# A two-column matmul of zeros ahead of each run of matmuls on the weights' low parts

## The chip, the cores and the metric

The kernel runs on one core of a Trainium2 chip. The metric is the device time of one execution in microseconds (us), from the first to the last instruction and a little around them; lower is better. Engines are named as in the profile: PE is TensorE's matmul side, PEld its weight loads (LDWEIGHTS), DVE is VectorE, ACT ScalarE, POOL GpSimd, SP the engine that issues most DMAs.

## The reference, cut to what matters

Two layers of a decoder trunk over 256 tokens and a model width of 2048. All products with weight matrices are in float32.

```
for l in range(DEPTH):                       # DEPTH = 2
    h = rms_norm(x, pre_mix_norm[l])
    p = h @ w_in[l]                          # 2048 x 5648: q, k, v, z, xbc, dt
    A = attention(q, k, v)                   # 8 heads x 128, causal, 256 tokens
    S = ssd_scan(silu(conv(xbc)), dt, ...)   # 16 heads x 64, state 128
    y = concat(rms_norm(A), rms_norm(S * silu(z))) @ w_out[l]     # 2048 x 2048
    x = x + rms_norm(y, post_mix_norm[l])
    h = rms_norm(x, pre_mlp_norm[l])
    h = square(relu(h @ w_up[l])) @ w_down[l]                     # 2048 x 8192, 8192 x 2048
    x = x + rms_norm(h, post_mlp_norm[l])
```

## The kernel before, in words

Every float32 value that goes through a large product is split in two parts: a high part (`w_hi`, `a_hi`, `u_hi`), rounded to TensorE's narrower float32 kind, and a low part that holds what the rounding left (`w_lo`, `a_lo`, `u_lo`). A product is then three: high weights by high activations, high weights by low activations, low weights by high activations, all added in PSUM.

The weights stream in as chunks of 128 x 1024 numbers, eight chunks to a block of 512 output columns, 47 blocks to a layer. SP loads a chunk into `raw`, ACT rounds it to `w_hi` (L549, semaphore `hi_ready`), DVE subtracts to make `w_lo` (L1288, semaphore `split_done`), PE multiplies and counts up `mm_done`, which frees the place. Four chunks are in flight (`RING`).

PE has three ways to work off a chunk:

- `token_chunk` (lines 832 to 834): activations are the stationary operand and 512 weight columns move past. High and low take turns, 128x512 each time. Blocks of v, z, w_out and w_down.
- `half_chunk` (L888, L895) for the q and k blocks and two of xbc, and `wide_chunk` (L937, L945) for the w_up blocks: the two-width blocks. The weights are stationary, 128x128 at a time, and the activations move. `a_both` holds the high and the low part of the activations side by side, so one matmul of 512 moving columns does high weights by both (L888, L937). The low weights need the high activations alone, 256 moving columns (L895, L945). A chunk has eight matmuls of each width.
- `feature_chunk`, for the first block of a layer.

In the two-width blocks an even chunk does its 8 wide matmuls first and then its 8 narrow ones; an odd chunk does narrow first and then wide. So PE alternates between 16 wide and 16 narrow matmuls. Each matmul has a weight load of its own, 128 columns. An even chunk waits for `split_done` (`take`) between its two halves.

Other work for PE (transposes, the state-space and attention products) is placed between the chunks by a table of slots; in the q, k and xbc blocks it often stands behind an even chunk, which cuts a run of 16 narrow matmuls into 8 and 8. The table and all other engines' programs are in a fixed order.

`wdt_both` is a tile of 608 columns of the narrower float32 kind: 512 hold the parts of the dt columns of w_in, and the last 96 are zeros, written once at the start by POOL.

Of the kernel before, what the change touches and what calls it, by code (L numbers as in the profile page):

```python
# [41 lines left out]
KT = D // P  # L42
# [3 lines left out]
SH, SP_, SG, SN, TAPS = 16, 64, 2, 128, 4  # L46
# [89 lines left out]
def trunk(nc, x, positions, pre_mix_norm, post_mix_norm, pre_mlp_norm, post_mlp_norm, w_in, conv_w,  # L136
          conv_b, dt_bias, a_log, d_skip, attn_out_norm, ssd_out_norm, w_out, w_up, w_down, out):
    ctx = ExitStack()
    with ctx:
        def sb(name, shape, dt=F32):  # L140
            return ctx.enter_context(nc.sbuf_tensor(name, shape, dt))
# [19 lines left out]
        wdt_both = sb("wdt_both", [P, 2 * KT * SH + P - 2 * SH], F32R)  # L161
# [30 lines left out]
        wide = [ctx.enter_context(nc.psum_tensor(f"wide{i}", [P, 4, CB], F32)) for i in range(2)]  # L192
# [82 lines left out]
        def chunk(b, c):  # L275

            return b * NC + c
# [534 lines left out]
        def _(pe):  # L812
# [9 lines left out]
            def take(b, c):  # L822

                pe.wait_ge(sem["split_done"], RING + 1 + chunk(b, c))
# [15 lines left out]
            def feature_chunk(c, par, first_ready=None, hi_ready=None, lo_ready=None):  # L840
# [32 lines left out]
                                        skip_group_check=True)  # L873
                ins.then_inc(sem["mm_done"], 1)

            def half_chunk(c, b):

                k, c4 = divmod(c, NC // 2)
                banks = acc[1 - k]

                def w(a, kk, m):
                    return a[:, c % RING, kk * SEQ + m * P:kk * SEQ + (m + 1) * P]

                def high_weights():
                    for kk in range(2 * CK):
                        kt = c4 * 2 * CK + kk
                        for m in range(2):
                            ins = pe.matmul(banks[m], w(w_hi_off, kk, m), a_both[:, kt].rearrange("p a s -> p (a s)"),  # L888
                                            start=(kt == 0), stop=(kt == KT - 1), skip_group_check=True)
                    return ins  # L890

                def low_weights():
                    for kk in range(2 * CK):
                        for m in range(2):
                            ins = pe.matmul(banks[m][:, 0:SEQ], w(w_lo_off, kk, m), a_hi[:, c4 * 2 * CK + kk],  # L895
                                            start=False, stop=False, skip_group_check=True)
                    return ins

                if c % 2 == 0:
                    pe.wait_ge(sem["hi_ready"], chunk(b, c) + 1)  # L900
                    high_weights()
                    take(b, c)
                    ins = low_weights()
                else:
                    take(b, c)
                    low_weights()
                    ins = high_weights()
                ins.then_inc(sem["mm_done"], 1)

            def wide_chunk(c, j, b, first_ready=None, hi_ready=None, lo_ready=None):  # L910


                def w(a, kk, m):
                    return a[:, c % RING, kk * CB + m * P:kk * CB + (m + 1) * P]

                if lo_ready:
                    take(b, c)
                    for kk in range(CK):
                        k = c * CK + kk
                        pe.wait_ge(*(hi_ready if kk else first_ready))  # L920
                        for m in range(CB // P):
                            pe.matmul(wide[j][:, m, 0:SEQ], w(w_hi_off, kk, m), a_hi[:, k], start=(k == 0), stop=False,
                                      skip_group_check=True)
                            pe.matmul(wide[j][:, m, 0:SEQ], w(w_lo_off, kk, m), a_hi[:, k], start=False, stop=False,
                                      skip_group_check=True)
                    pe.wait_ge(*lo_ready)
                    for kk in range(CK):
                        for m in range(CB // P):
                            ins = pe.matmul(wide[j][:, m, SEQ:2 * SEQ], w(w_hi_off, kk, m), a_lo[:, c * CK + kk],
                                            start=False, stop=False, skip_group_check=True)  # L930
                    ins.then_inc(sem["mm_done"], 1)
                    return
                def high_weights():
                    for kk in range(CK):
                        k = c * CK + kk
                        for m in range(CB // P):
                            ins = pe.matmul(wide[j][:, m], w(w_hi_off, kk, m), a_both[:, k].rearrange("p a s -> p (a s)"),  # L937
                                            start=(k == 0), stop=(k == KT - 1), skip_group_check=True)
                    return ins

                def low_weights():
                    for kk in range(CK):
                        k = c * CK + kk
                        for m in range(CB // P):
                            ins = pe.matmul(wide[j][:, m, 0:SEQ], w(w_lo_off, kk, m), a_hi[:, k], start=False, stop=False,  # L945
                                            skip_group_check=True)
                    return ins

                if c % 2 == 0:
                    pe.wait_ge(sem["hi_ready"], chunk(b, c) + 1)
                    high_weights()
                    take(b, c)
                    ins = low_weights()
                else:
                    take(b, c)
                    low_weights()
                    ins = high_weights()
                ins.then_inc(sem["mm_done"], 1)  # L960

            for l in range(DEPTH):
# [201 lines left out]
                for slot in range(MIX_SLOTS):  # L1164
# [18 lines left out]
                    if b == 0:  # L1183
                        feature_chunk(c, 0, *(() if slot else first_waits(0)))
                    elif b < B_V:
                        half_chunk(c, l * NB + b)
                    elif b < B_OUT:
                        token_chunk(c, acc[b % 2], a_hi, a_lo)
                    else:
                        last_half = slot >= MIX_SLOTS - NC // 2  # L1190
                        token_chunk(c, acc[b % 2], u_hi, u_lo, (0,) if last_half else range(TT))
                        if slot == MIX_SLOTS - 1:

                            for c in range(NC // 2, NC):
                                token_chunk(c, acc[b % 2], u_hi, u_lo, (1,))
# [31 lines left out]
                def up_pair(q, i):  # L1227
                    for j in range(2):
                        first = j == 0 and is_first(q, i)
                        if first:  # L1230
                            first_turns(1, WARM_UP, M[3])
                            pe.wait_ge(*left(l, B_OUT + 2, 2))
                            pe.wait_ge(*left(l, B_OUT + 3, 2))
                        pe.wait_ge(*up_left(l, j, q * (QB // 2) + i, 0))
                        pe.wait_ge(*down_left(l, j, q * (QB // 2), 0))
                        for c in range(NC):
                            b = l * NB + q * (2 * QB) + i * 2 + (B_MLP + j)
                            hi_first = first and c == 0
                            if not hi_first:
                                pe.wait_ge(*upto("xT_ready", l, 8 + c + 1))  # L1240
                            wide_chunk(c, j, b, *(first_waits(1) if hi_first else ()))
                            if first:
                                for jj in NORM_PE.get(c, ()):
                                    x_turn(1, jj)
# [551 lines left out]
```

## Time and profile before

| | before |
|---|---|
| median of 3 runs | 2194.89 us (2194.66 to 2195.25) |
| the profiled execution | 2195.13 us |
| its span, first to last instruction | 2193.4 us |
| PE busy | 2174.4 us (99%), 11454 matmuls |
| PEld busy | 1867.7 us (85%), 11454 loads |
| DVE busy | 1360.5 us (62%) |
| ACT busy | 1022.7 us (47%) |
| DMA engines | 404.30 MB, mean 184 GB/s |
| granted TensorE clock | 0.999 of full speed, the 2.4 GHz level |

Matmuls overlap: one of 512 columns is shown as 389 ns long, but the next starts some 227 ns after it. So the durations say little of the rate, and starts are to be compared: in the timeline a row that merges n equal instructions begins at the start of the first, and the row of what follows on the same engine begins n steps later. The profile before and after it is one execution each; its own time is compared with its own span.

### The profile page before, as it was taken

Reading aid. Unit: us, or ns where it says so; the run is one execution under the profiler, and the core shown is the slowest. Engines: PE = TensorE matmul, PEld = TensorE weight load, DVE = VectorE, ACT = ScalarE, POOL = GpSimd, SP = SyncE. Lnnn points to the kernel's source line nnn. Section 1 sums busy time; section 2 is a strip of 40 time slices with the busy share of each in tenths; the row PEclk is TensorE's granted clock in tenths of the full one; section 3 lists DMA queues with packets and bytes.
Section 4 is the critical chain, followed back from the end, with each engine's and each line's share of the span. In section 5 each row is a group of like instructions: output and inputs, shape, how many; then the busy total and the mean of one; then the engine's idle time right before and its main releaser. Section 6 shows DMA issues by size and latency. Waiting matters only on the chain.

```text
span 2193.4 us, 32256 instructions
## 1 busy us (share of the span) xinstructions
PE 2174.4 (99%) x11454; PEld 1867.7 (85%) x11454; DVE 1360.5 (62%) x1633; ACT 1022.7 (47%) x1313; POOL 112.7 (5%) x107
## 2 busy tenths in 40 slices
PE   8999999999999999999999999999999999999998
PEld 8888888888888888888898888888888888888886
DVE  6977464764555465556588875657555655554655
ACT  6544464643444344344455444546434434443443
POOL 2051000000000000000001510000000000000000
PEclk9999999999999999999999999999999999999999
DMA  6655556656665656665556555556666566656564
GB/s 211 181 153 166 159 187 197 191 177 207 184 195 195 190 180 202 191 189 190 182 157 184 152 172 149 198 182 188 205 193 192 172 209 176 204 194 192 174 206 148
DMA packets 232312, 404.30 MB, mean 184 GB/s; under 512 B 12492, under 2 KB 61924, under 8 KB 231716
## 3 DMA queue, kind: packets, MB, share of 16 engines
q1 hardware_dynamic: 230420, 396.47, 58.7%
q10 hardware_dynamic: 1264, 5.31, 0.6%
q0 software_dynamic: 544, 1.38, 0.3%
q8 instruction: 56, 0.92, 0.2%
q14 instruction: 28, 0.23, 0.0%
HBM read 401.01 MB, written 2.10 MB: 184 GB/s over the span
## 4 chain that ended last, share of the span: by engine, by line
PE 94%; DVE 3%; issue 1%; POOL 1%; ACT 1%; DMA 0%; POOLq 0%; DVEq 0%; ACTq 0%
PE wide L937 21%; PE wide L832 16%; PE wide L834 16%; PE wide L833 16%; PE wide L945 11%; PE wide L888 6%; PE wide L895 3%; DVE w_lo L1288 1%; PE wide L869 1%; PE wide L871 1%; PE wide L872 1%; PE wide L1075 1%; PE wide L976 1%; POOL u_lo L500 0%; POOL u_hi L500 0%
## 5 line engine op out<-in xcount | busy, mean ns | idle before, releaser
L1288 DVE TENSOR_TENSOR w_lo<-raw,w_hi 128x1024 fp32r<-128x1024 f32 x752 | 923.5, 1237 | 709.1 <-ACT w_hi L549 664.3
L549 ACT ACTIVATE w_hi<-raw 128x1024 fp32r<-128x1024 f32 x752 | 788.2, 1058 | 893.0 <-PE wide L834 488.0
L832 PE MATMUL wide<-w_hi,u_hi 128*128 128x512 f32 x1280 | 498.5, 389 | 0.0
L834 PE MATMUL wide<-w_hi,u_lo 128*128 128x512 f32 x1280 | 498.0, 389 | 0.0
L833 PE MATMUL wide<-w_lo,u_hi 128*128 128x512 f32 x1280 | 497.9, 389 | 0.0
L937 PE MATMUL wide<-a_both,w_hi 128*128 128x512 f32 x2032 | 486.3, 391 | 0.0
L937 PEld LDWEIGHTS wide<-a_both,w_hi 128*128 128x128 f32 x2032 | 373.2, 188 | 72.1
L834 PEld LDWEIGHTS wide<-w_hi,u_lo 128*128 128x128 f32 x1280 | 240.2, 188 | 50.0
L833 PEld LDWEIGHTS wide<-w_lo,u_hi 128*128 128x128 f32 x1280 | 240.3, 188 | 49.7
L832 PEld LDWEIGHTS wide<-w_hi,u_hi 128*128 128x128 f32 x1280 | 240.2, 188 | 49.6
L945 PEld LDWEIGHTS wide<-a_both,w_lo 128*128 128x128 f32 x2032 | 257.3, 189 | 9.6
L945 PE MATMUL wide<-a_both,w_lo 128*128 128x256 f32 x2032 | 261.1, 281 | 0.0
L888 PE MATMUL wide<-a_both,w_hi 128*128 128x512 f32 x768 | 186.4, 393 | 0.0
L888 PEld LDWEIGHTS wide<-a_both,w_hi 128*128 128x128 f32 x768 | 140.4, 188 | 27.7 <-issue 1.0
L895 PEld LDWEIGHTS wide<-a_both,w_lo 128*128 128x128 f32 x768 | 100.0, 189 | 6.1 <-issue 1.0
L895 PE MATMUL wide<-a_both,w_lo 128*128 128x256 f32 x768 | 103.5, 282 | 0.0
L832 PE MATMUL wide<-w_hi,a_both 128*128 128x512 f32 x256 | 102.6, 401 | 0.0
L834 PE MATMUL wide<-w_hi,a_both 128*128 128x512 f32 x256 | 100.0, 391 | 0.0
L833 PE MATMUL wide<-w_lo,a_both 128*128 128x512 f32 x256 | 99.8, 390 | 0.0
L480 POOL TENSOR_TENSOR st<-st,minus_half 128x1 f32<-128x1 f32 x8 | 4.4, 547 | 1539.3 <-DVE st L1368 1539.3
L768 ACT ACTIVATE u_hi<-wk 128x512 f32 (+1 forms) x64 | 39.5, 632 | 49.5 <-DVE wk L1696 49.5
L1690 DVE TENSOR_TENSOR wk<-wide,wk 128x512 f32<-128x512 f32 x64 | 41.2, 686 | 31.8 <-ACT wk L760 31.8
(248 smaller groups left out, 1367.1 us busy)
## 6 DMA issues: line engine op xcount, KB each, us to landing
raw<-in_w_up SPq DMA_DIRECT2D x256, 512.0 KB, 3.8
raw<-in_w_down SPq DMA_DIRECT2D x256, 512.0 KB, 4.5
raw<-in_w_in SPq DMA_DIRECT2D x176, 512.0 KB, 3.7
raw<-in_w_out SPq DMA_DIRECT2D x64, 512.0 KB, 4.4
zg<-in_post_mix_norm ACTq DMA_DIRECT2D x2, 1024.0 KB, 4.7
zg<-in_post_mlp_norm ACTq DMA_DIRECT2D x2, 1024.0 KB, 7.5
out<-x_sb SPq DMA_DIRECT2D x8, 256.0 KB, 2.5
x_sb<-in_x ACTq DMA_DIRECT2D x2, 512.0 KB, 8.6
```

The costliest lines, as they stand in the source:

```text
L549: act.activation(w_hi[:, c % RING], raw[:, c % RING], ACT.Copy).then_inc(sem["hi_ready"], 1)
L768: act.activation(u.rearrange("p k s -> p (k s)"), wk[:, 2 + k], ACT.Copy)\
L832: pe.matmul(o, sh, wh, start=(k == 0), stop=False)
L833: pe.matmul(o, sh, wl, start=False, stop=False)
L834: ins = pe.matmul(o, sl, wh, start=False, stop=(k == KT - 1))
L869: pe.matmul(o(m), w(w_hi, kk, m), a_hi[:, k], start=(k == 0 and m % 2 == 0), stop=False, skip_group_check=True)
L888: ins = pe.matmul(banks[m], w(w_hi_off, kk, m), a_both[:, kt].rearrange("p a s -> p (a s)"), start=(kt == 0), stop=(kt == KT - 1), skip_gr ...
L895: ins = pe.matmul(banks[m][:, 0:SEQ], w(w_lo_off, kk, m), a_hi[:, c4 * 2 * CK + kk], start=False, stop=False, skip_group_check=True)
L937: ins = pe.matmul(wide[j][:, m], w(w_hi_off, kk, m), a_both[:, k].rearrange("p a s -> p (a s)"), start=(k == 0), stop=(k == KT - 1), skip_ ...
L945: ins = pe.matmul(wide[j][:, m, 0:SEQ], w(w_lo_off, kk, m), a_hi[:, k], start=False, stop=False, skip_group_check=True)
L1288: dve.tensor_tensor(lo[:, c % RING], raw[:, c % RING], hi[:, c % RING].bitcast(F32), ALU.subtract).then_inc(sem["split_done"], 1)
L1690: dve.tensor_tensor(wk[:, k].rearrange("p (m s) -> p m s", m=2), wide[j][:, 2 * k:2 * k + 2, 0:SEQ], wk[:, k].rearrange("p (m s) -> p m s" ...
```

## The change

A helper `add_zero` issues one more matmul. Both operands are the same two columns of zeros of `wdt_both`, so the result is a 2 x 2 block of zeros, added to two rows and two columns of a PSUM bank that the running product already uses; what is computed stays the same. It is called for every even chunk of the two-width blocks, behind the 8 wide matmuls and behind the wait for `split_done`, ahead of the first narrow matmul.

```
+            def add_zero(bank):
+
+                zero = wdt_both[:, 2 * KT * SH:2 * KT * SH + 2]
+                pe.matmul(bank[0:2, 0:2], zero, zero, start=False, stop=False, skip_group_check=True)
+
             def half_chunk(c, b):
...
                     pe.wait_ge(sem["hi_ready"], chunk(b, c) + 1)
                     high_weights()
                     take(b, c)
+                    add_zero(banks[0])
                     ins = low_weights()
...
                     high_weights()
                     take(b, c)
+                    add_zero(wide[j][:, 0])
                     ins = low_weights()
```

PE's order of work in the first half block (the xbc block behind the first one) of a layer, before: L1006 and L1007 are the dt product, L888 the wide and L895 the narrow matmuls, L1014 a transpose.

```order
L1006 MATMUL wide<-a_both,wdt_both 128x256
L1007 MATMUL wide<-a_both,wdt_both 128x256
L888 MATMUL wide<-a_both,w_hi 128x512 x8
L895 MATMUL wide<-a_both,w_lo 128x256 x16
L888 MATMUL wide<-a_both,w_hi 128x512 x16
L895 MATMUL wide<-a_both,w_lo 128x256 x8
L1014 MATMUL wide<-ident,wk 128x128 x2
L895 MATMUL wide<-a_both,w_lo 128x256 x8
```

The same place now; all lines below `add_zero` have moved by 5 to 7 (L893 is the wide matmul, L900 the narrow one, L879 the new one):

```order
L1013 MATMUL wide<-a_both,wdt_both 128x256
L1014 MATMUL wide<-a_both,wdt_both 128x256
L893 MATMUL wide<-a_both,w_hi 128x512 x8
L879 MATMUL wide<-wdt_both 2x2
L900 MATMUL wide<-a_both,w_lo 128x256 x16
L893 MATMUL wide<-a_both,w_hi 128x512 x16
L879 MATMUL wide<-wdt_both 2x2
L900 MATMUL wide<-a_both,w_lo 128x256 x8
L1021 MATMUL wide<-ident,wk 128x128 x2
L900 MATMUL wide<-a_both,w_lo 128x256 x8
```

Nothing changes places; one matmul with its own weight load comes in ahead of each run, and where other work cuts a run in two, ahead of its first part alone. The same holds in the w_up blocks, here at the turn from one block to the next (PSUM tile wide0 to wide1; L943 wide, L951 narrow):

```order
L943 MATMUL wide0<-a_both,w_hi 128x512 x16
L879 MATMUL wide0<-wdt_both 2x2
L951 MATMUL wide0<-a_both,w_lo 128x256 x16
L943 MATMUL wide0<-a_both,w_hi 128x512 x8
L943 MATMUL wide1<-a_both,w_hi 128x512 x8
L879 MATMUL wide1<-wdt_both 2x2
L951 MATMUL wide1<-a_both,w_lo 128x256 x16
```

A layer has 6 half blocks with 4 even chunks each, and 16 w_up blocks with 4 each; in one of the latter, the first of the layer, the first chunk has another form without the new matmul. That makes 24 + 63 = 87 a layer and 174 in all. Followed through the program's order, 26 of the 48 in the half blocks and 2 of the 126 in the w_up blocks stand ahead of a run that other work cuts after its first 8 matmuls; the other 146 stand ahead of 16. No other engine's instructions change.

## Rows read from the trace of the kernel before

**Rows 1.** The page: busy time and instructions; then the chain's shares.
```profile
PE 2174.4 (99%) x11454; PEld 1867.7 (85%) x11454; DVE 1360.5 (62%) x1633; ACT 1022.7 (47%) x1313; POOL 112.7 (5%) x107
...
PE 94%; DVE 3%; issue 1%; POOL 1%; ACT 1%; DMA 0%; POOLq 0%; DVEq 0%; ACTq 0%
```

**Rows 2.** Waits of PE, longest first: us in total, times, longest us.
```profile
PE wide L819 <- DMA wk<-in_ssd_out_norm: 2.6, 1, 2.6
```

**Rows 3.** Groups: line, engine, operation, count | busy, mean ns | idle before.
```profile
L937 PE MATMUL wide<-a_both,w_hi 128*128 128x512 f32 x2032 | 486.3, 391 | 0.0
L945 PE MATMUL wide<-a_both,w_lo 128*128 128x256 f32 x2032 | 261.1, 281 | 0.0
```

**Rows 4.** Timeline of PE, w_up block, a wide run: start, us, engine, line, operation, count.
```profile
749.45 3.82 PE L937 MATMUL wide<-a_both,w_hi 128*128 128x512 f32 x16
753.10 2.05 PE L945 MATMUL wide<-a_both,w_lo 128*128 128x256 f32 x16
```

**Rows 5.** Timeline of both sides at one change from wide to narrow.
```profile
747.34 0.41 PEld L945 LDWEIGHTS wide<-a_both,w_lo 128*128 128x128 f32 x2
747.56 0.40 PE L945 MATMUL wide<-a_both,w_lo 128*128 128x256 f32 x2
```

**Rows 6.** Timeline of PEld, loads for matmuls of 64 moving columns.
```profile
137.19 0.97 PEld L1075 LDWEIGHTS wide<-x_tok,wk 128*128 128x128 f32 x8 [1.37 <-DVE wk L1541]
138.08 0.19 PEld L1062 LDWEIGHTS wide<-u_hi,low 128*128 128x128 f32 x1
```

**Rows 7.** Timeline of PEld, loads for matmuls of 16 moving columns and the next.
```profile
71.02 0.30 PEld L1022 LDWEIGHTS wide<-dts,tri 128*128 128x128 f32 x2
71.24 0.30 PEld L888 LDWEIGHTS wide<-a_both,w_hi 128*128 128x128 f32 x2
```

**Rows 8.** Timeline, narrow run behind transposes, half block: PE before it, both during it.
```profile
78.72 1.11 PE L895 MATMUL wide<-a_both,w_lo 128*128 128x256 f32 x8
79.66 0.60 PE L1030 MATMUL wide<-ident,xbcT 128*128 128x128 f32 x4
80.01 1.17 PE L895 MATMUL wide<-a_both,w_lo 128*128 128x256 f32 x8
81.02 0.40 PE L888 MATMUL wide<-a_both,w_hi 128*128 128x512 f32 x1
...
79.99 0.99 PEld L895 LDWEIGHTS wide<-a_both,w_lo 128*128 128x128 f32 x8
```

**Rows 9.** Timeline of PE, a narrow run of 16 soon behind other work.
```profile
114.30 2.42 PE L888 MATMUL wide<-a_both,w_hi 128*128 128x512 f32 x8
116.56 1.98 PE L895 MATMUL wide<-a_both,w_lo 128*128 128x256 f32 x16
118.37 3.81 PE L888 MATMUL wide<-a_both,w_hi 128*128 128x512 f32 x16
122.02 0.28 PE L895 MATMUL wide<-a_both,w_lo 128*128 128x256 f32 x1
```

**Rows 10.** The first and the last of 12 narrow parts behind transposes: first load, next matmul.
```profile
51.41 1.00 PEld L895 LDWEIGHTS wide<-a_both,w_lo 128*128 128x128 f32 x8
...
52.45 0.40 PE L888 MATMUL wide<-a_both,w_hi 128*128 128x512 f32 x1
...
1489.63 1.00 PEld L945 LDWEIGHTS wide<-a_both,w_lo 128*128 128x128 f32 x8
...
1490.67 0.40 PE L937 MATMUL wide<-a_both,w_hi 128*128 128x512 f32 x1
```

**Rows 11.** The first and the last of 146 narrow runs of 16, and what follows.
```profile
44.81 2.05 PE L895 MATMUL wide<-a_both,w_lo 128*128 128x256 f32 x16
46.70 0.63 PE L888 MATMUL wide<-a_both,w_hi 128*128 128x512 f32 x2
...
2094.27 2.05 PE L945 MATMUL wide<-a_both,w_lo 128*128 128x256 f32 x16
2096.16 1.09 PE L937 MATMUL wide<-a_both,w_hi 128*128 128x512 f32 x4
```

More of the change, by code:

```diff
@@ L874, in feature_chunk, with add_zero @@
                 ins.then_inc(sem["mm_done"], 1)
+            def add_zero(bank):
+                zero = wdt_both[:, 2 * KT * SH:2 * KT * SH + 2]
+                pe.matmul(bank[0:2, 0:2], zero, zero, start=False, stop=False, skip_group_check=True)
             def half_chunk(c, b):
@@ L902, in half_chunk @@
                     take(b, c)
+                    add_zero(banks[0])
                     ins = low_weights()
@@ L954, in wide_chunk @@
                     take(b, c)
+                    add_zero(wide[j][:, 0])
                     ins = low_weights()
```

## The prediction

> **What bounds the kernel now.** I read the page's busy line and chain first. PE is busy 99% of the span and the chain that ended last lies on PE for 94% of it [rows 1]. Then PE's waits: the longest in the whole run is 2.6 us at the start, and none of the listed ones is for `w_hi` or `w_lo` [rows 2]. So the other engines and the DMAs are ahead of PE, and the time is the sum of PE's steps from one matmul to the next. The w_up blocks alone have 2032 wide and 2032 narrow matmuls [rows 3]. What matters is not how long a matmul is shown but how soon the next starts, so I go on to the timelines.
>
> In a w_up block a wide run of 16 takes 753.10 - 749.45 = 3.65 us, 228 ns a step [rows 4], and a narrow run of 16 takes 2096.16 - 2094.27 = 1.89 us, 118 ns a step [rows 11]. Where wide turns to narrow, the first narrow matmul starts at 747.56, so the last wide one started a step before, at 747.33; the weight load for the narrow one starts at 747.34 [rows 5]: a load goes out when the matmul ahead of it starts, not earlier. There is one load in flight ahead of the array and no second.
>
> **The change part by part.** It adds 174 matmuls with a load each, and removes and moves nothing. The wait for `split_done` now hangs on the new matmul's load instead of the first narrow one's; PE does not wait there [rows 2], so this costs nothing. If that cover were gone, the wait would be as long as before, since nothing else is queued between.
>
> Step 1, the new load. It goes out when the last wide matmul starts and has the 227 ns of that matmul to itself; a load of 128 columns takes half of that (below). Nothing.
>
> Step 2, the new matmul, and this is the cost. It is over at once, but the load of the first narrow weights, all 128 columns, may start only when it starts, and it has nothing to hide behind. No row shows a matmul of two columns. The nearest are those whose moving side is shorter than a load. With 64 columns, eight loads take 138.08 - 137.19 = 0.89 us, 111 ns each, as the loads follow each other without a gap [rows 6]. With 16 columns, two loads take 71.24 - 71.02 = 0.22 us, 110 ns each [rows 7]. Four times fewer columns change nothing, so I take 112 ns for two columns too. From below the bound is the shortest step between two recorded starts, some 28 ns from the last transpose (79.66 and three steps of 0.109) to the first narrow matmul at 80.01, whose load starts at 79.99 [rows 8]. That is a start that is recorded as soon as its own load has begun; the time comes back in the next step. From above, nothing in the rows says that a short matmul costs more than its follower's load.
>
> Step 3, the narrow run behind it. The trace shows two paces for the same instruction. Behind a settled wide run it is 118 ns [rows 11]. But in another place a run of 16 takes 118.37 - 116.56 = 1.81 us, 113 ns a step [rows 9]: there other work stood only eight wide matmuls ahead. And behind transposes, where the first narrow load is not hidden any more, 8 narrow matmuls take 81.02 - 79.99 = 1.03 us from that load's start [rows 8]. There are twelve such places, of which [rows 10] has the first (52.45 - 51.41 = 1.04) and the last (1490.67 - 1489.63 = 1.04); their mean is 1.036 us, and in all twelve the step is down at 113 to 114 ns by the eighth matmul. If the pace were 118 to the end, it would be 0.112 + 8 x 0.118 = 1.06. So a run whose first load is exposed falls into the quicker pace within a few steps. I expect the same behind the new matmul, since it exposes the same load.
>
> That gives, from the start of the new matmul: 1.036 us for 8 narrow ones, plus 8 x 0.1133 = 0.907 for the other 8, 1.943 in all, against a mean of 1.886 over the 146 full runs before ([rows 11] has the first and the last, 1.89 each). So +0.057 us for each: +8.3 us. Where other work cuts the run after 8, it is 1.036 against 79.66 - 78.72 = 0.94 [rows 8]: +0.092 for each of 28: +2.6 us.
>
> Step 4, the wide run behind it. It takes 3.65 us in the w_up blocks, where narrow runs are slow [rows 4, 11], and 122.02 - 118.37 = 3.65 behind a quick one [rows 9]. Nothing.
>
> Step 5, the other engines. PE gets later, they keep their slack. Nothing.
>
> Sum: +10.9 us on the profiled execution's 2195.13 us (span 2193.4 and 1.7 around it), 2206.0. That execution lies 0.24 above the median of the runs, so I say 2205.8 us.
>
> A page of the Trainium skill speaks against this cost. "TensorE: Matmul & The Clock Gate", section "Back-to-back issue gap", puts one to 64 columns at about 60 cycles, some 25 ns. By that the new matmul would cost 25 ns and the quicker pace would win it back, 2188 us. That is rival B's time, reached in another way. This case's trace does not agree: the loads of its short matmuls stand 111 ns apart [rows 6].
>
> **The rivals.**
>
> A: the run stays at 118 ns. The quicker pace might need a break of another kind: all twelve places have a float32 transpose or product ahead, not a matmul of zeros of the narrower kind. For it: the pace is not a matter of the instruction alone, as two runs in [rows 9, 11] show. Against it: twelve out of twelve. Then each new matmul costs its 113 ns and gives nothing: 174 x 0.113 = 19.7 us, 2214.6 us.
>
> B: the load is hidden, faster than before. If PE could load the narrow weights while the last wide matmul still runs (the new load is only two columns, so two loads would fit into 227 ns), the new matmul would cost only the 28 ns of the shortest recorded step, and the run would start at the quick pace. Price: 1.886 - 1.813 - 0.028 = 0.045 us saved for 146 and 0.944 - 0.907 - 0.028 = 0.009 for 28, 6.8 us, 2188.1. It decides the sign from the point where the exposed part of the load is under 73 ns. Against it: no load in the stretches that I read begins before the matmul ahead of it, even with the array busy for 227 ns more [rows 5].
>
> C: a bit of both, the exposed part near 73 ns, so that pace and load cancel: 2191 to 2199.
>
> D: the narrow output makes the array empty itself ahead of the new matmul and again behind it. A wide matmul is shown 391 ns long [rows 3] with a step of 228 [rows 4], so emptying is 163 ns at most; twice that and the exposed load, 2 x 0.163 + 0.112 = 0.44 us, is 76 us over 174, about 2271. All matmuls in the rows use the full 128*128, so no row shows it or excludes it. The page "TensorEngine Tiling (Array Packing)", section "Key Properties", says that changing the tiling mode drains TensorE; no row here shows a change of mode.
>
> **How the numbers follow.** Forecast 0.64, A 0.16, B 0.09, C 0.07, D 0.04. The likeliest case's own range is 2202 (the quick pace from the first step: 0.039 and 0.075 us, 7.8 us) to 2209. The range for 8 in 10 takes in rival A: 2200 to 2216. A measurement of this kernel tells about 0.2%, 4.4 us, from no change. Faster by more than that: B, 0.09. Within it: C, 0.07. Slower: the rest, 0.84.
>
> **What would show it.** A new group of 174 matmuls; start of the new matmul to start of the next load 2 to 4 ns, and from that load to the end of the run 1.94 us. If the run behind the new matmul takes 1.81 us and the new step 28 ns, B is right; if the run's last steps are 118 ns, A. Weight loads that begin ahead of the matmul before them would make step 2 wrong. A wide run other than 3.65 us would break step 4. A wait of PE for `w_lo` would break step 5.

## The result, and the profile after

The changed kernel takes 2204.73 us (median of 6 runs, 2204.25 to 2206.2) against 2194.86 (6 runs): the ratio is 1.0045, with a 95% interval of 1.0035 to 1.0055. It is slower by 9.9 us, where 10.9 was predicted; the time lies in the range and in the forecast's own. The profiled execution took 2205.03 us, 9.9 more than the one before, with a span of 2203.3.

The page and the groups of the changed kernel, as [rows 1, 3] (line, engine, operation, count | busy, mean ns | idle before; L951 is the narrow matmul of the w_up blocks, L879 the new one; the wide one, L943, has 486.2 us, as good as unchanged):

```profile
PE 2187.0 (99%) x11628; PEld 1861.9 (85%) x11628; DVE 1361.4 (62%) x1633; ACT 1023.8 (46%) x1313; POOL 111.8 (5%) x107
...
L951 PE MATMUL wide<-a_both,w_lo 128*128 128x256 f32 x2032 | 263.9, 282 | 0.0
...
L879 PE MATMUL wide<-wdt_both 128*2 128x2 f32 x174 | 28.9, 166 | 0.0
...
L879 PEld LDWEIGHTS wide<-wdt_both 128*2 128x2 f32 x174 | 14.4, 83 | 6.8
```

174 more matmuls, and no new idle time of PE. The 166 ns and 28.9 us of the new group are not its price: it overlaps its neighbours as all matmuls do. Its place is read from the timeline (start, us, engine, line, operation, count):

```profile
751.21 0.17 PE L879 MATMUL wide<-wdt_both 128*2 128x2 f32 x1
751.24 2.07 PE L951 MATMUL wide<-a_both,w_lo 128*128 128x256 f32 x16
753.15 3.81 PE L943 MATMUL wide<-a_both,w_hi 128*128 128x512 f32 x16
756.80 0.17 PE L879 MATMUL wide<-wdt_both 128*2 128x2 f32 x1
```

and the last wide matmul ahead of the first of these places, with the weight loads from there on:

```profile
750.99 0.39 PE L943 MATMUL wide<-a_both,w_hi 128*128 128x512 f32 x1
...
750.99 0.08 PEld L879 LDWEIGHTS wide<-wdt_both 128*2 128x2 f32 x1
751.22 1.90 PEld L951 LDWEIGHTS wide<-a_both,w_lo 128*128 128x128 f32 x16
```

The new matmul's own load starts at 750.99, with the last wide matmul, and is hidden. The first narrow load waits for the new matmul: 751.22 behind 751.21. From the new matmul to the wide run it is 753.15 - 751.21 = 1.94 us, where the run alone took 1.89 [rows 11]. The wide run takes 756.80 - 753.15 = 3.65, as in [rows 4].

Step by step, the trace at full resolution shows 27, 202, 118, and from the third narrow matmul on 113 and 114 ns in 142 of the 146 full runs; the run takes 1.907 us and the new matmul's own step 0.027. Added up from start to start over the whole trace, the new matmul's steps take 4.8 us and the narrow runs 4.9 us more (L951 +2.7, L900 +2.2): 9.7 of the 9.9 us.

Four full runs stay at 118 ns. All four have other work only eight wide matmuls ahead, and a wide run that has not settled when they start (its last steps are 231, 236 and 228 ns, where those of a settled run are 227). The first of them:

```profile
90.58 2.10 PE L893 MATMUL wide<-a_both,w_hi 128*128 128x512 f32 x8
92.52 0.16 PE L879 MATMUL wide<-wdt_both 128*2 128x2 f32 x1
92.55 2.13 PE L900 MATMUL wide<-a_both,w_lo 128*128 128x256 f32 x16
94.52 0.40 PE L893 MATMUL wide<-a_both,w_hi 128*128 128x512 f32 x1
```

94.52 - 92.55 = 1.97 us, 118 ns a step behind the first. In the kernel before it was a place of this kind that had the quick pace [rows 9].

Nor is the change confined to the runs behind the new matmul. Twelve narrow parts stand behind transposes or other short products, with their first load exposed, and all twelve reached the quick pace in the kernel before [rows 8, 10]. In the changed kernel three do, and nine stay at 118 ns. The first of them, and its loads:

```profile
51.79 0.38 PE L1021 MATMUL wide<-ident,wk 128*128 128x128 f32 x2
51.93 1.19 PE L900 MATMUL wide<-a_both,w_lo 128*128 128x256 f32 x8
52.95 0.40 PE L893 MATMUL wide<-a_both,w_hi 128*128 128x512 f32 x1
...
51.90 1.01 PEld L900 LDWEIGHTS wide<-a_both,w_lo 128*128 128x128 f32 x8
```

The first narrow load starts 26 ns ahead of its matmul and the next load 109 ns later, in both kernels, so it is exposed as before. From that load the part takes 52.95 - 51.90 = 1.05 us instead of 1.04, and its last three steps are 119, 117 and 120 ns instead of 114, 113 and 113. The nine take 1.054 us on average, where the twelve took 1.034 before. It costs only 0.2 us in all, but it says that an exposed load does not bring the quick pace by itself.

### The profile page after: what moved, and what is told of

Same layout as the page of the kernel before. It is cut to its first block, busy times and chain, and to the rows that moved or that the text cites. A ratio compares the mean times of both kernels' runs of the same rounds, so it can differ in the third digit from the quotient of the medians.

```text
span 2203.3 us, 32604 instructions
## 1 busy us (share of the span) xinstructions
PE 2187.0 (99%) x11628; PEld 1861.9 (85%) x11628; DVE 1361.4 (62%) x1633; ACT 1023.8 (46%) x1313; POOL 111.8 (5%) x107
## 4 chain that ended last, share of the span: by engine, by line
PE 94%; DVE 3%; issue 1%; POOL 1%; ACT 1%; DMA 0%; ACTq 0%; POOLq 0%; DVEq 0%
PE wide L943 21%; PE wide L832 16%; PE wide L834 16%; PE wide L833 16%; PE wide L951 11%; PE wide L893 5%; PE wide L900 3%; DVE w_lo L1295 1%; PE wide L869 1%; PE wide L871 1%; PE wide L872 1%; PE wide L1082 1%; POOL u_lo L500 1%; PE wide L983 1%; DMA x_sb<-in_x 0%
## 5 line engine op out<-in xcount | busy, mean ns | idle before, releaser
L943 PE MATMUL wide<-a_both,w_hi 128*128 128x512 f32 x2032 | 486.2, 391 | 0.0
L943 PEld LDWEIGHTS wide<-a_both,w_hi 128*128 128x128 f32 x2032 | 372.0, 188 | 72.2
L951 PE MATMUL wide<-a_both,w_lo 128*128 128x256 f32 x2032 | 263.9, 282 | 0.0
L951 PEld LDWEIGHTS wide<-a_both,w_lo 128*128 128x128 f32 x2032 | 241.1, 188 | 17.9
L893 PE MATMUL wide<-a_both,w_hi 128*128 128x512 f32 x768 | 186.3, 393 | 0.0
L893 PEld LDWEIGHTS wide<-a_both,w_hi 128*128 128x128 f32 x768 | 140.2, 188 | 27.8 <-issue 1.0
L900 PE MATMUL wide<-a_both,w_lo 128*128 128x256 f32 x768 | 106.2, 285 | 0.0
L900 PEld LDWEIGHTS wide<-a_both,w_lo 128*128 128x128 f32 x768 | 95.2, 188 | 9.2 <-issue 1.0
```

## The experiments

The questions: is the price the exposed load of the first narrow weights, and nothing of the new matmul itself? Does the exposed load bring the quick pace, or would anything in that place? Is there a cheaper way to it? Line numbers differ by a few from kernel to kernel; the operands tell which matmul it is.

**64 moving columns instead of 2** (of the changed kernel).

```
-                pe.matmul(bank[0:2, 0:2], zero, zero, ...)
+                moving = wdt_both[:, 2 * KT * SH:2 * KT * SH + 64]
+                pe.matmul(bank[0:2, 0:64], zero, moving, ...)
```

> The new matmul moves 64 columns of zeros instead of 2; all else as in the changed kernel. Theory (the price is the load behind it, 112 ns, whatever the matmul itself moves): the matmul's own 27 ns of columns are still under that load, so the time stays at 2204.7 us, within 0.1%, and the run behind it stays at 113 ns a step. Rival (the price grows with its own columns): 62 more columns are 26 ns, times 174 is 4.5 us, 2209.2 us.

Measured 2204.72 us, ratio to the kernel before 1.0044 (1.0027 to 1.0061).

```profile
750.94 0.19 PE L880 MATMUL wide<-wdt_both 128*2 128x64 f32 x1
750.97 2.07 PE L952 MATMUL wide<-a_both,w_lo 128*128 128x256 f32 x16
752.88 2.46 PE L944 MATMUL wide<-a_both,w_hi 128*128 128x512 f32 x10
```

1.94 us from the new matmul to the wide run, as with 2 columns. Its own columns cost nothing: the load behind sets the price.

**96 output rows instead of 2.**

```
-                pe.matmul(bank[0:2, 0:2], zero, zero, ...)
+                wide_zero = wdt_both[:, 2 * KT * SH:2 * KT * SH + 96]
+                pe.matmul(bank[0:96, 0:2], wide_zero, zero, ...)
```

> The new matmul has 96 zero columns as weights instead of 2 (output 96 x 2); all else as in the changed kernel. Theory (its own load is hidden under the last wide matmul, and a narrow output costs nothing special): 2204.7 us, within 0.1%. Rival (a load of two columns is what keeps the price at 112 ns, and a full one in front of another full one costs more): 80 ns more each, 14 us, 2218.6 us. Rival (the narrow output itself costs, as the array is set up for few rows and back): faster than 2204.7 by more than 2 us.

Measured 2204.68 us, ratio 1.0044 (1.0027 to 1.006). Its own load, now 96 columns, is hidden as well:

```profile
750.97 0.16 PEld L880 LDWEIGHTS wide<-wdt_both 128*96 128x96 f32 x1
751.19 1.90 PEld L952 LDWEIGHTS wide<-a_both,w_lo 128*128 128x128 f32 x16
```

The narrow output is free, and rival D of the prediction is out: no place shows the 0.33 us that emptying the array twice would take, with 2 rows or with 96.

**256 moving columns**, so that the new matmul covers the load behind it.

```
-                pe.matmul(bank[0:2, 0:2], zero, zero, ...)
+                pe.matmul(bank[0:2, 0:SEQ], zero, a_hi[:, 0], ...)
```

> The new matmul still has the two zero columns as weights, but moves 256 columns (the high parts of the activations). Now its own columns cover the load behind it. It takes at least as long as that load, so the step stays at some 113 ns; what tells is the pace behind it. Theory (the quick pace comes from a load that stands exposed): nothing is exposed, the run stays at 118 ns, and the 174 matmuls cost 113 ns each with no return: 2214.6 us. Rival (any additional step between the wide and the narrow run brings the quick pace): 146 x (0.113 - 0.073) + 28 x (0.113 - 0.037) = 8.0 us, 2203 us.

Measured 2214.36 us, ratio 1.0088 (1.0071 to 1.0105): the theory's number within 0.3 us.

```profile
753.69 0.28 PE L879 MATMUL wide<-a_both,wdt_both 128*2 128x256 f32 x1
753.81 2.05 PE L951 MATMUL wide<-a_both,w_lo 128*128 128x256 f32 x16
755.69 3.81 PE L943 MATMUL wide<-a_both,w_hi 128*128 128x512 f32 x16
```

755.69 - 753.81 = 1.88 us: the slow pace. The new matmul's step is 0.12 us, about what the exposed load cost, and without an exposed load nothing comes back: 144 of the 146 full runs are slow. This is what rival A would have cost, and it shows that one more matmul in that place is not by itself what brings the quick pace.

**The last wide matmul in two halves**, of the kernel before: one more step and nothing exposed.

```
+                if c % 2 == 0 and <last of the eight>:
+                    for part in range(2):
+                        pe.matmul(<bank>[:, part * SEQ:(part + 1) * SEQ], w(w_hi_off, kk, m), a_both[:, k, part], ...)
+                    continue
```

> The kernel before without the new matmul; instead the last of the 16 wide matmuls ahead of each narrow run is done as two of 256 columns with the same weights, which are loaded twice. Each half covers one load, so it should cost 0 to 14 ns a place (2 x 113 or 2 x 120 against 227). Theory (only an exposed load brings the quick pace): the runs stay at 118 ns, 2195 to 2197.3 us. Rival (any additional step shifts the two sides against each other and brings the quick pace): 146 x 0.073 + 28 x 0.037 less, 2183.2 to 2185.6 us, faster than both kernels.

Measured 2196.7 us, ratio 1.0008 (0.9998 to 1.0017).

```profile
748.45 0.40 PE L945 MATMUL wide<-a_both,w_hi 128*128 128x256 f32 x2
748.69 2.05 PE L957 MATMUL wide<-a_both,w_lo 128*128 128x256 f32 x16
750.57 1.78 PE L949 MATMUL wide<-a_both,w_hi 128*128 128x512 f32 x7
```

The run takes 1.88 us, the slow pace again, as all 146 do; the theory holds.

**The same new matmul ahead of the wide runs instead.**

```
                     take(b, c)
-                    add_zero(banks[0])
                     ins = low_weights()
...
                     low_weights()
+                    add_zero(banks[0])
                     ins = high_weights()
```

> The same two-column matmul, moved from the head of each narrow run to the head of each wide run (176 places). Theory (price: whatever load stands behind it is exposed; return: only the run right behind gets another pace): narrow runs are back at 118 ns and 1.887 us; the load of the first wide matmul is exposed, 112 ns; the wide run may lose its unsettled first steps (27 ns). 176 x (0.085 to 0.119) us, 2210 to 2216 us. Rival (the quick pace lasts once it is there, wherever the exposed load was): narrow runs at 113 ns, 2204 us or less.

Measured 2214.35 us, ratio 1.0087 (1.007 to 1.0104).

```profile
754.56 2.04 PE L951 MATMUL wide<-a_both,w_lo 128*128 128x256 f32 x16
756.44 0.17 PE L879 MATMUL wide<-wdt_both 128*2 128x2 f32 x1
756.47 3.90 PE L943 MATMUL wide<-a_both,w_hi 128*128 128x512 f32 x16
760.20 0.99 PE L951 MATMUL wide<-a_both,w_lo 128*128 128x256 f32 x7
```

Narrow runs are back at 756.44 - 754.56 = 1.88 us, and the wide run with the new matmul takes 760.20 - 756.44 = 3.76 instead of 3.65: an exposed load costs 0.11 us there too, and the pace of the run behind it is its own matter. Sixteen settled wide matmuls later nothing of it is left.

**Two of them ahead of each narrow run.**

```
                     take(b, c)
                     add_zero(banks[0])
+                    add_zero(banks[0])
```

> Two of the two-column matmuls stand ahead of each narrow run instead of one. Theory (what costs is the load of 128 columns behind the last of them; a load of two columns is short): the second adds only a shortest step of about 28 ns, 174 x 0.028 = 4.9 us on 2204.7, 2209.6 us. Rival (each matmul with a load behind it costs 112 ns whatever is loaded): 2224.2 us. On the pace: theory, the runs stay at 113 ns, since the load of the first narrow weights is exposed as before; rival, the second one sets it back to 118, 13 us more.

Measured 2207.71 us, ratio 1.0058 (1.0041 to 1.0075), 3.0 us above the changed kernel, where the theory had 4.9.

```profile
751.51 0.19 PE L879 MATMUL wide<-wdt_both 128*2 128x2 f32 x2
751.56 2.06 PE L952 MATMUL wide<-a_both,w_lo 128*128 128x256 f32 x16
753.46 3.81 PE L944 MATMUL wide<-a_both,w_hi 128*128 128x512 f32 x16
```

1.95 us in all. The second one costs its step of 26 ns and not 112: a load of two columns behind a matmul is cheap, one of 128 is what costs. Part of the 26 comes back: the quick pace is there one matmul earlier (the step of 118 is now 114), and it is there in all 174 places, also in the six that stayed slow behind a single new matmul, although the load of 128 columns is exposed in both kernels alike.

**Wide and narrow in turns**, of the kernel before, one by one and then by fours (an even chunk waits for both parts first).

```
-                    high_weights() ... low_weights()      # runs of 16
+                    for kk, m in ...:
+                        pe.matmul(<wide, w_hi>)
+                        pe.matmul(<narrow, w_lo>)
```

> The kernel before, but wide and narrow matmuls take turns in the two-width blocks (each even chunk waits for its low parts before its first matmul). Theory one (every load is covered by the matmul ahead, and the slow pace needs a settled wide run ahead of a run of narrow ones): a pair takes 227 + 113 ns, 16 pairs 5.44 us against 5.54, 17 us less, 2178 us. Rival (each turn from narrow to wide costs what the first steps of a wide run cost, 6 to 10 ns, and narrow stays at 118): a pair takes 351 ns, 5.62 us, 14 us more, 2209 us.

Measured 2197.13 us, ratio 1.0009 (0.9999 to 1.0018): between the two, 19 us above the theory and 12 below the rival.

```profile
750.05 0.39 PE L954 MATMUL wide<-a_both,w_hi 128*128 128x512 f32 x1
750.28 0.28 PE L956 MATMUL wide<-a_both,w_lo 128*128 128x256 f32 x1
...
751.44 0.39 PE L954 MATMUL wide<-a_both,w_hi 128*128 128x512 f32 x1
```

Four pairs take 1.39 us, 347 ns each: narrow 117, wide 230. Neither pace is reached for good.

> The kernel before, with four wide and four narrow matmuls in turn in the two-width blocks (an even chunk waits for its low parts first). The first five steps of a wide run are unsettled (233, 236, 228, 232, 231 ns), from the sixth on they are 227. Theory (a narrow run that is entered from an unsettled wide run has the quick pace, as the few such places in the trace of before show): 929 + 4 x 113.3 = 1382 ns for four pairs against 1385 before, 2193 us. Rival (with the load covered the run is at 118 ns): 929 + 472 = 1401, 11 us more, 2206 us.

Measured 2205.3 us, ratio 1.0047 (1.003 to 1.0064).

```profile
750.78 1.09 PE L956 MATMUL wide<-a_both,w_hi 128*128 128x512 f32 x4
751.71 0.64 PE L959 MATMUL wide<-a_both,w_lo 128*128 128x256 f32 x4
752.18 1.09 PE L956 MATMUL wide<-a_both,w_hi 128*128 128x512 f32 x4
```

752.18 - 750.78 = 1.40: the rival is right and my theory of this run is wrong. The wide run is unsettled (0.93 for four) and yet the narrow one behind it has 118 ns. So an unsettled wide run is not enough for the quick pace; in [rows 9] there was other work eight matmuls ahead, and here there is none.

**The offset of the low parts** in the two-width blocks, 16 columns before, now 8, 32 and 48.

```
-SHIFT, ROOM = 16, 128
+SHIFT, ROOM = 8, 128
```

> The kernel before, with the low parts of the weights in the two-width blocks lying 8 columns further than the ring's start instead of 16. Theory (the two paces are two ways in which the load of w_lo and the moving columns can lie against each other, and where w_lo lies sets which are possible): the narrow step changes, to 113 ns for good (2183 us) or to the 120 ns that the first block's matmuls of 256 columns show without an offset (2800 x 0.002 us more, 2201 us). Rival (the pace is a matter of the order of loads and matmuls alone): 118 ns, 2194.9 us within 0.1%.

> As the kernel with 8 columns, with 32. Theory: the narrow step changes from 118 ns, down to 113 (2183 us) or up to 120 (2201 us). Rival: 118 ns, 2194.9 us within 0.1%.

> The kernel before, low parts of the weights 48 columns off in the two-width blocks (16 before; 8 and 32 gave 2200.8 and 2200.2 us). Theory (where w_lo lies against the moving columns counts in steps of 32 columns, so 48 is like 16): 2195 us within 0.1%. Rival (16 is special): 2200 us or more.

Measured 2200.83 us (1.0026, 1.0017 to 1.0036), 2200.2 (1.0024, 1.0014 to 1.0033) and 2200.28 (1.0024, 1.0014 to 1.0034). With 8 columns:

```profile
751.39 3.84 PE L937 MATMUL wide<-a_both,w_hi 128*128 128x512 f32 x16
755.07 2.05 PE L945 MATMUL wide<-a_both,w_lo 128*128 128x256 f32 x16
756.96 0.40 PE L937 MATMUL wide<-a_both,w_hi 128*128 128x512 f32 x1
```

and with 32:

```profile
751.09 3.81 PE L937 MATMUL wide<-a_both,w_hi 128*128 128x512 f32 x16
754.73 2.08 PE L945 MATMUL wide<-a_both,w_lo 128*128 128x256 f32 x16
756.65 0.62 PE L937 MATMUL wide<-a_both,w_hi 128*128 128x512 f32 x2
```

The place counts, but not in the way that was expected. With 8 the narrow run keeps 1.89 us and the wide one takes 3.68 instead of 3.65; with 32 the wide one keeps 3.64 and the narrow one takes 1.92; 48 is like 8, not like 16. None brings runs of 113 ns.

**A load that is exposed by a little**, of the kernel before: the last wide matmul as 288 and 224 columns. 224 columns run for less than a load takes.

```
+                if c % 2 == 0 and <last of the eight>:
+                    for lo, hi in ((0, 288), (288, 512)):
+                        pe.matmul(<bank>[:, lo:hi], w(w_hi_off, kk, m), <a_both[:, k], 512 columns>[:, lo:hi], ...)
+                    continue
```

> The kernel before without the new matmul; the last wide matmul ahead of each narrow run is done as one of 288 and one of 224 columns with the same weights, loaded twice. The 224 columns take 99 ns, 13 less than the load of 112 ns behind them, so that load stands exposed by 13 ns instead of 112. Theory (what brings the quick pace is that the run is entered behind an exposed load, even a little exposed, as behind the transposes with 109 ns against 112): narrow runs at 113 ns; 146 x (0.073 - 0.013 - 0.005) + 28 x (0.037 - 0.018) = 8.6 us less, 2186.4 us. Rival (the load must be exposed by its whole length, or the settled wide run carries its state over a small gap): 118 ns stay and the gap is paid, 174 x 0.013 = 2.3 us more, 2197.2 us.

Measured 2189.96 us (2189.61 to 2190.4, 11 runs), ratio 0.9978 (0.9969 to 0.9987): 4.9 us faster than the kernel before and 14.8 faster than the changed one.

```profile
746.34 0.40 PE L945 MATMUL wide<-a_both,w_hi 128*128 128x288 f32 x2
746.57 2.00 PE L957 MATMUL wide<-a_both,w_lo 128*128 128x256 f32 x16
748.41 3.59 PE L949 MATMUL wide<-a_both,w_hi 128*128 128x512 f32 x15
...
746.47 1.91 PEld L957 LDWEIGHTS wide<-a_both,w_lo 128*128 128x128 f32 x16
```

The run takes 748.41 - 746.57 = 1.84 us instead of 1.89, at 113 ns from its sixth step. At the wide run's rate 224 columns take 227 x 224 / 512 = 99 ns; the step is 107, so the load behind, which starts at 746.47 with that part, is exposed by 8 ns. The two parts ahead of it take 128 + 107 = 235 ns against 227 for the undivided one. That is 0.047 saved and 0.008 paid on 142 full runs, 5.5 us (4 take 1.90). The theory had 8.6 us: its direction is right, but it allowed 5 ns for the way to the quick pace, and the first four steps (122, 118, 122 and 116) take some 25 more than four at 113. The halves of 256 columns differ from this only in where the matmul is divided, so that its last part covers the load, and they have the slow pace in every run. So behind a settled wide run a load exposed by 8 ns goes with the quick pace nearly as well as one exposed by 112. That it is the exposure, and not the 2 ns by which the narrow run starts later than behind the halves (235 against 233) or the unequal size of the parts, is argued and not shown: no run divides the matmul unequally with a last part that still covers the load.

**The twelve places behind other work, in all kernels.** They have the same exposed load everywhere, and the traces of the runs above show their pace. In the four kernels whose full narrow runs are slow they are quick in 43 of 48 cases (12 of 12 before, 12 with the new matmul ahead of the wide runs, 10 with the halves, 9 with 256 columns). In the five whose full runs are quick it is 18 of 60 (3 in the changed kernel, 4 with 64 columns, 4 with 96 rows, 2 with two new matmuls, 5 with 288 and 224). Ten of the twelve stand behind a first narrow part of their own. Where that part was slow, the part behind the other work is quick in 34 of 44 cases; where it was quick, in 14 of 46. So an exposed load more often changes the pace than brings the quick one, and neither holds in every case.

## Why the prediction was right

- Step 1, the new load is hidden: it starts at 750.99 with the last wide matmul, also with 96 columns.
- Step 2, the price is the load of the next 128 columns: with 2 and with 64 moving columns the second narrow matmul starts 111 ns later than it would, and with 256, where the new matmul covers the load, 117. Only the two-column load behind it, with two new matmuls in a row, is cheap. The prediction set a figure of the Trainium skill against this price, some 25 ns for a matmul of 1 to 64 columns ("TensorE: Matmul & The Clock Gate", section "Back-to-back issue gap"). That section gives it for a matmul without a load to wait for and says that in a stream of loads and matmuls both set the spacing, so it did not speak against the price. The traces agree with it: 26 ns where the load behind has two columns, 111 where it has 128.
- Step 3, the quick pace behind the exposed load: right in 142 of 146 full runs and in 26 of the 28 cut ones. It comes sooner than in the twelve places of [rows 8, 10]: 1.934 us from the new matmul to the end instead of 1.943. The four runs at 118 ns work the other way with 4 x 0.05 = 0.2 us. Together the full runs cost 7.3 us instead of 8.3.
- The reason given for step 3 was too strong, and here luck had a part. It rested on twelve places out of twelve, and in the changed kernel nine of the same twelve stay slow behind the same exposed load. Behind settled wide runs, which is where nearly all of the new matmuls stand, the rule held; as a rule for any exposed load it does not. The twelve also average 1.034 us at full resolution where the sum has 1.036.
- The cut runs cost 2.1 us instead of 2.6, 0.4 of it because the other work behind them waits less. The nine places add 0.2 us, a term that the sum did not have. With the 7.3 that makes, before rounding, the 9.7 us found above; the rest of the 9.9 lies outside the two-width blocks' narrow runs.
- Steps 4 and 5: the wide run has its 3.65 us, and PE waits for no weights.
- Rival B, the hidden load, is excluded by 751.22 behind 751.21, and D by the 96 output rows. A is excluded for this kernel by the 142 runs at 113 ns; its price of 113 ns a place was measured with 256 columns, as 118 ns and 2214.36 us. C has no run that speaks for it.

What was not foreseen either is the flip of the few runs that start behind an unsettled wide run with other work at its head. In the kernel before, the four of them that there are (two full, two cut) have the quick pace; with the new matmul there are six (four full, two cut) and none has it. They are too few to move the sum. What such a wide run carries from the other work over eight matmuls, and no longer over sixteen, stays open: the fours show that its unsettled steps alone are not it. Whether these six have one cause with the nine places behind other work is open too; in six of the nine the narrow part ahead had the quick pace. Equally open is what the two paces are physically; the offsets show that it matters where `w_lo` lies, no more.

## What to carry to other kernels

A matmul that is shorter than the load behind it costs that load: on an engine that never waits, the two-column instruction here cost the whole load of the next 128 columns, 112 ns, and not its own step of 27. The same instruction can run at two paces (113 and 118 ns) for reasons that lie ahead of it, so look at the steps between starts, run by run, and at the exceptions, before pricing a change. A rule read from twelve places out of twelve can still hang on what stands ahead of them: check it in the kernel after as well. Where a small disturbance brings the better pace, look for the smallest that does: splitting a matmul that is there anyway cost 8 ns where the extra one cost 112.

## What the runs showed of the hardware

- Loads of two columns are shown as 83 ns long, of 96 as 160 and of 128 as 188. Where nothing covers them, they hold the matmuls up by far less: 26 ns for two columns (two new matmuls in a row) and 110 to 112 for 128.
- A float32 operand of the narrower kind moves at 113.3 ns for 256 columns and 226.7 for 512, at the 2.4 GHz level (granted clock 0.998 to 0.999); that is 272 and 544 clocks of that level. The wide run's first five steps behind a narrow run are longer (233, 236, 228, 232, 231) in the kernel before and in the changed one, where the low parts lie 16 columns off; with 32 they are 232, 231, 228, 227 and 227.
- An exposed first load goes with the quick pace in 168 of the 174 new places, and in 3 of the 12 places behind other work in the same kernel.
- The offset of one operand by 8, 32 or 48 columns instead of 16 costs 5 to 6 us over the kernel: 26 to 28 ns in each wide run with 8 or 48 columns, 2 ns at each narrow step with 32.
